# A hybrid RWKV/NSA decoder step: one ring of weight buffers for three stages, and a down projection with the weights stationary

## What is computed

```
h  = RMSNorm(x) * (1 + scale1(c)) + shift1(c)
P  = h @ w_in            # RWKV-7 columns | NSA columns | two merge gates (2 x 1024 columns)
yA = RWKV7(P_rwkv) @ w_pa ;  yB = NSA(P_nsa) @ w_pb
x  = x + gate1(c) * ((sigmoid(gA) * yA + sigmoid(gB) * yB) @ w_o)
h2 = RMSNorm(x) * (1 + scale2(c)) + shift2(c)
val, gate = split(h2 @ ffn_w_up)          # 1024 -> 2 x 2816
f  = (silu(conv3(gate)) * val) @ ffn_w_down   # 2816 -> 1024
x  = x + gate2(c) * f
```

## Time and profile before

| | us |
|---|---|
| median of 3 runs | 2840.73 |
| the profiled execution | 2833.18 |
| its span | 2831.5 |
| first merge matmul | 1534.13 |
| first up matmul | 2000.81 |
| first down matmul | 2524.47 |
| start of the last down matmul | 2828.37 |

### The profile page before, as it was taken

How to read it: one execution, slowest core, us unless ns; L and a number is a source line. 1 busy time by engine, 2 the same in 40 slices (tenths; PEclk the granted TensorE clock), 3 DMA queues, 4 the chain that set the end, 5 groups by cost and what they waited for, 6 DMA issues and landing times. The chain is left out here.

```text
span 2831.5 us, 47908 instructions
## 1 busy us (share of the span) xinstructions
PE 2524.0 (89%) x20071; PEld 2054.6 (73%) x20071; DVE 1179.9 (42%) x2457; ACT 699.4 (25%) x1400; POOL 384.2 (14%) x284
## 2 busy tenths in 40 slices
PE   4896998999857898989986999999799999979999
PEld 2675885454434676868585888744799999979999
DVE  5331224555512444435363011134233333359998
ACT  3231124566411213222222000011111111113333
POOL 3001200000120000000002111000222233223320
PEclk6897987999868989999997999999899999989999
DMA  7434411101332000000002101031211111122210
GB/s 266 183 135 133 140 35 43 31 1 46 105 119 76 17 6 24 7 23 3 12 3 102 27 26 31 9 126 55 57 50 49 45 45 45 45 95 73 70 49 16
DMA packets 150472, 171.45 MB, mean 61 GB/s; under 512 B 14089, under 2 KB 135242, under 8 KB 147762
## 3 DMA queue, kind: packets, MB, share of 16 engines
q1 hardware_dynamic: 144626, 152.66, 16.7%
q0 software_dynamic: 5632, 15.74, 1.9%
HBM read 155.47 MB, written 17.05 MB: 61 GB/s over the span
## 5 line engine op out<-in xcount | busy, mean ns | idle before, releaser
L173 PE MATMUL pP_u<-h_hi,w_up_hi 128*128 128x352 f32 x1056 | 341.5, 323 | 11.8 <-POOL w_up_lo L167 11.8
L174 PE MATMUL pP_u<-h_lo,w_up_hi 128*128 128x352 f32 x1056 | 339.2, 321 | 0.0
L175 PE MATMUL pP_u<-h_hi,w_up_lo 128*128 128x352 f32 x1056 | 338.8, 321 | 0.0
L173 PE MATMUL pP_d<-w_down_hi,a_piece_hi 128*128 128x256 f32 x792 | 226.4, 286 | 31.1 <-DVE a_piece_lo L2911 31.1
L174 PE MATMUL pP_d<-w_down_lo,a_piece_hi 128*128 128x256 f32 x792 | 225.3, 284 | 0.0
L175 PE MATMUL pP_d<-w_down_hi,a_piece_lo 128*128 128x256 f32 x792 | 225.1, 284 | 0.0
L173 PEld LDWEIGHTS pP_u<-h_hi,w_up_hi 128*128 128x128 f32 x1056 | 198.8, 188 | 11.9 <-POOL w_up_lo L167 11.9
L174 PEld LDWEIGHTS pP_u<-h_lo,w_up_hi 128*128 128x128 f32 x1056 | 199.0, 188 | 0.0
L175 PEld LDWEIGHTS pP_u<-h_hi,w_up_lo 128*128 128x128 f32 x1056 | 198.5, 188 | 0.0
L1584 PE MATMUL pB_e<-hT,w_rwkv 128*128 128x352 f32 x576 | 182.3, 473 | 16.7 <-DVE rw_slots L1608 9.5
L2801 DVE TENSOR_TENSOR conv<-conv,conv_sig 128x1056 f32<-128x1056 f32 x22 | 50.4, 2289 | 322.8 <-ACT conv_sig L2769 322.8
(11 more groups left out here) (468 smaller groups left out, 4741.5 us busy)
## 6 DMA issues: line engine op xcount, KB each, us to landing
w_up<-in_w_up SPq DMA_DIRECT2D x44, 512.0 KB, 4.1
ybT<-in_w_ada SPq DMA_DIRECT2D x9, 2048.0 KB, 7.6
kv_ring<-in_pool_kv SPq DMA_DIRECT2D x80, 128.0 KB, 2.1
xt<-in_x SPq DMA_DIRECT2D x16, 512.0 KB, 3.7
cx<-in_pool_c POOLq DMA_DIRECT2D x64, 128.0 KB, 3.0
cx<-in_pool_c SPq DMA_DIRECT2D x64, 128.0 KB, 2.9
w_gate<-in_w_in SPq DMA_DIRECT2D x16, 512.0 KB, 4.2
w_rwkv<-in_w_in SPq DMA_DIRECT2D x14, 512.0 KB, 4.1
```

The costliest lines, as they stand in the source:

```text
L173: nc.tensor.matmul(out, w_hi, x_hi, start=start, stop=False)
L174: nc.tensor.matmul(out, w_hi, x_lo, start=False, stop=False)
L175: return nc.tensor.matmul(out, w_lo, x_hi, start=False, stop=stop)
```

## The change

One set of buffers (`w_raw` for what a transfer brings, `w_hi` and `w_lo` for the parts, two slots of 128 x 1024 each) is made before the last RWKV stage, in the memory that some RWKV tensors held before. The gate blocks are numbers 0 to 15 of one sequence, the up blocks 16 to 59 (`UP0`), the down blocks from 60 on (`DOWN0`). Load n waits until block n-2 is split; the split of n waits until PE has used n-2, or stands in a stage that begins after that.

Blocks 0 and 1 are loaded and split in the last RWKV stage. Merge loads blocks 2 to 17 and splits 2 to 16; out_proj splits 17 and loads 18 and 19; up loads 20 to 61 and splits 18 to 60; down does the rest.

In the down projection blocks of 128 x 128 weights are stationary and 352 tokens stream past. A quarter of 256 columns is two halves of 128, and it is cut in 6 parts (five of 4 blocks of FF, one of 2). A piece is a part and 352 tokens; there are 72. The sums of a quarter stay in 6 PSUM banks over its 6 parts. They come out as columns by tokens, so ACT copies them to SBUF (`f_cols`), PE transposes them, two 128 x 128 blocks to an output of 256 columns (a turn), and DVE multiplies by the gate and adds. A turn stands after each half piece in the first two parts of the next quarter; the nine turns of the last quarter stand at the end. The gate rows are waited for at the first output.

```diff
+def load_block(sp, S, n, source):
+    if n >= 2:
+        sp.wait_ge(S["w_split"], 2 * (n - 1))
+    rows, width = source.shape[1:]
+    dst = S["w_raw"][:, n % 2, 0:rows * width].rearrange("p (k n) -> p k n", n=width)
+    sp.dma_start(dst, source).then_inc(S["w_in"][n % 2], 16)
+
+def split_block(nc, pool, S, n, size=1024):
+    pool.wait_ge(S["w_in"][n % 2], 16 * (n // 2 + 1))
+    x = slice(0, size)
+    split(nc, nc.gpsimd, S["w_raw"][:, n % 2, x], S["w_hi"][:, n % 2, x], S["w_lo"][:, n % 2, x], S["w_split"], 2 * n)
+
+UP0, DOWN0 = 16, 16 + 2 * FC
+DOWN_Q = 256
+DOWN_PART = [(0, 4), (4, 8), (8, 12), (12, 16), (16, 20), (20, 22)]
...
 # last stage of rwkv
                 @block.sync
                 def _(sp):
+                    for g in range(2):
+                        load_block(sp, S, g, gate_block(A, g))
                     sp.dma_start(O["shift"], R["last"][:, :, :]).then_inc(done, 16)
                     sp.wait_ge(done, 16)
+
+                @block.gpsimd
+                def _(pool):
+                    for g in range(2):
+                        split_block(nc, pool, S, g)
 # merge
-                sp.dma_start(WG[:, 0], A["w_in"][:, :, G0:G0 + 128]).then_inc(wg_in[0], 16)
                 for w, n in enumerate(("w_pa", "w_pb")):
                     sp.dma_start(WP[:, w], A[n]).then_inc(wp_in, 16)
-                for g in range(1, 16):
...
+                for g in range(2, 16):
+                    load_block(sp, S, g, gate_block(A, g))
+                for n in range(2):
+                    load_block(sp, S, UP0 + n, up_block(A, n))
...
+                for g in range(2, 17):
+                    pool.wait_ge(mm, 2 * (g - 2) + 1)
+                    split_block(nc, pool, S, g)
 # out_proj
                 for i in range(10):
+                    if i in (4, 6):
+                        load_block(sp, S, UP0 + i // 2, up_block(A, i // 2))
...
+            @block.gpsimd
+            def _(pool):
+                split_block(nc, pool, S, UP0 + 1)
 # ffn_up
+                for n in range(4, 2 * FC):
+                    load_block(sp, S, UP0 + n, up_block(A, n))
+                for n in range(2):
+                    load_block(sp, S, DOWN0 + n, down_block(A, n))
...
+                for n in range(2, 2 * FC + 1):
+                    pool.wait_ge(mm, n - 1)
+                    split_block(nc, pool, S, UP0 + n)
 # ffn_down, order of the turns
+        for m, (n, i) in enumerate(pieces):
+            h, k = chunks[n]
+            for half in range(2):
+                turn_after[m, half] = waiting.pop(0) if waiting else None
+            if k == 0 and h:
+                waiting += [9 * (h - 1) + 3 * i + c for c in range(3)]
+        last_turns = list(range(9 * (NQ - 1), 9 * NQ))
 # ffn_down, POOL
+                for n, (h, k) in enumerate(chunks[1:], 1):
+                    if n == 1:
+                        pool.wait_ge(S["up_mm"], 2 * FC)
+                    else:
+                        pool.wait_ge(mm, 3 * (n - 1))
+                    split_block(nc, pool, S, DOWN0 + n, Q * (PART[k][1] - PART[k][0]))
 # ffn_down, ACT, after the hi part of piece m
+                    if m >= 2 and chunks[pieces[m - 2][0]][1] == NK - 1:
...
+                        nc.scalar.activation(fT[:, j % 3, :, :], pP[:, i, :, 0:PIECE], ACT.Copy).then_inc(evicted, 1)
 # ffn_down, PE
+                def turn(r):
+                    j, (c0, w) = r // 3, CUTS[r % 3]
+                    pe.wait_ge(evicted, j + 1)
+                    if r >= 2:
+                        pe.wait_ge(gated, r - 1)
+                    for half in range(2):
+                        last = nc.tensor.transpose(pT[0:w, r % 2, 128 * half:128 * half + 128], fT[:, j % 3, half, c0:c0 + w], S["ident"])
+                    last.then_inc(turned, 1)
...
+                    for half in range(2):
+                        for f in range(b - a):
+                            last = split_product(nc, pP[:, i, half, 0:PIECE], block_part(S, DOWN0 + n, Q * f + 128 * half),
+                                                 [x[:, m % 3, f, :] for x in AR], k == 0 and f == 0, k == NK - 1 and f == b - a - 1)
+                        if half == 1:
+                            last.then_inc(mm, 1)
+                        if turn_after[m, half] is not None:
+                            turn(turn_after[m, half])
+                for r in last_turns:
+                    turn(r)
 # ffn_down, DVE
+                for m, (n, i) in enumerate(pieces):
+                    if m >= 2:
+                        for half in range(2):
+                            if turn_after[m - 2, half] is not None:
+                                output(turn_after[m - 2, half])
...
+                    nc.vector.tensor_tensor(AR[1][:, m % 3, 0:b - a, :], aT[:, a:b, PIECE * i:PIECE * i + PIECE],
+                                            AR[0][:, m % 3, 0:b - a, :].bitcast(F32), ALU.subtract).then_inc(lo_done, 1)
+                for r in last_turns:
+                    output(r)
```

More of the change, by code:

```diff
@@ L2713, in ffn_up @@
         pP = ctx.enter_context(nc.psum_tensor("pP_u", [128, 2, 3, 512], F32))
-        w_in = [sem(f"wup_in{k}") for k in range(2)]
-        w_split = sem("wup_split")
-        prev_in, zero, mm, gate_in, val_in, conv, sig, act_done, chain = (
-            sem(f"fu_{n}") for n in ("prev", "zero", "mm", "gate", "val", "conv", "sig", "done", "chain"))
+        mm = S["up_mm"] = sem("fu_mm")
+        prev_in, zero, gate_in, val_in, conv, sig, act_done, chain = (
+            sem(f"fu_{n}") for n in ("prev", "zero", "gate", "val", "conv", "sig", "done", "chain"))
         par = S["par"]
@@ L2844, in store_rows @@
                 def store_rows(h):
-                    for i, (t0, m) in enumerate(TILES):
-                        sp.wait_ge(added, NT * (4 * h + 3) + i + 1)
-                        sp.dma_start(y[t0:t0 + m, h * Q:(h + 1) * Q], rows[0:m, h % 2, i, :]).then_inc(S[f"y_out{h % 2}"], 16)
+                    for r in range(9):
+                        sp.wait_ge(added, 9 * h + r + 1)
+                        c0, w = CUTS[r % 3]
+                        t0 = PIECE * (r // 3) + c0
+                        sp.dma_start(y[t0:t0 + w, h * Q:(h + 1) * Q], rows[0:w, h % 2, r, :]).then_inc(S[f"y_out{h % 2}"], 16)
@@ L2857, in _ @@
                         load_rows(0)
                         load_rows(1)
-                    if k == 3 and h >= 1:
+                    if k == NK - 1 and h >= 1:
                         store_rows(h - 1)
@@ L2891, in _ @@
                     if i == 0:
-                        pe.wait_ge(w_split, 2 * (n + 1))
-                    if m >= 8:
-                        pe.wait_ge(gated, m - 7)
+                        pe.wait_ge(S["w_split"], 2 * (DOWN0 + n + 1))
+                    if k == 0 and h:
+                        pe.wait_ge(evicted, 3 * (h - 1) + i + 1)
                     pe.wait_ge(lo_done, m + 1)
-                    for f in range(b - a):
-                        last = split_product(nc, pP[:, m % 8, 0:Q], [x[:, m % 3, f, :] for x in AR],
-                                             [x[:, n % 3, f, :] for x in WR], f == 0, f == b - a - 1)
@@ new lines, in output @@
+                def output(r):
+                    j, w = r // 3, CUTS[r % 3][1]
+                    h = j // 3
+                    gate = gates[1 if r % 9 == 8 else 0][0:w, h * Q:(h + 1) * Q]
+                    if r == 0:
+                        dve.wait_ge(gate_in, 48)
+                    if r % 9 == 0:
+                        dve.wait_ge(x_in[h % 2], 48 * (h // 2 + 1))
+                    dve.wait_ge(turned, r + 1)
+                    if r >= 2:
+                        dve.wait_ge(added, r - 1)
+                    nc.vector.tensor_tensor(gated_rows[0:w, r % 2, :], pT[0:w, r % 2, 0:Q], gate, ALU.mult).then_inc(gated, 1)
+                    dve.wait_ge(gated, r + 1)
+                    x = rows[0:w, h % 2, r % 9, :]
+                    nc.vector.tensor_tensor(x, gated_rows[0:w, r % 2, :], x, ALU.add).then_inc(added, 1)
```

177 lines of the change are left out of this document (76 added, 101 removed).

## The result

| | runs | median us | lowest to highest |
|---|---|---|---|
| before | 4 | 2841.62 | 2837.29 to 2843.26 |
| changed | 4 | 2774.72 | 2773.57 to 2783.27 |

The ratio is 0.977 (95% interval 0.9751 to 0.9796): 66.9 us less, where 60.2 were forecast. Five more runs on another chip had a median of 2774.90 us and a ratio of 0.9771 (0.9758 to 0.9784).

What follows compares the result with a forecast made beforehand. PE, busy 89% of the span, and its idle holes before merge, up and down were taken as the bound. Gains 12.8 + 8.6 + 6.0 + 39.4 less 6.6 make 60.2 us: 2840.7 to 2780.5, said as 2780, range 2769 to 2793.

Steps and rivals of the forecast that it cites:

- merge start: First merge matmul near 1520.8 instead of 1534.13, with gate blocks loaded and split a stage early: 13.3 us gained.
- given back in the first gate block: In merge, PE may wait for the second w_pab transfer: 0 to 1.2 us lost, taken as 0.5.
- up start: First up matmul near 1992.2 instead of 2000.81, with the first up blocks split earlier: 8.6 us gained.
- down start: First down subtraction no longer behind the gate rows, but stretched 0 to 2.3 us by POOL (1.4 taken): 6.0 us gained.
- down's body: Down's matmul stream with weights stationary: 264.8 us instead of 304.2, 39.4 us gained.
- end: After down's last matmul, nine turns and nine outputs remain: 9.5 us instead of 2.85, 6.6 us lost.
- 27 turns: Pairs of transposes inside down's matmul stream: 5.9 to 15.1 us in all, taken as 0.3 each, 8.1 us.
- three collisions and three quarter starts: In down, POOL splits meeting an output and its subtraction (1 us each), late quarter starts (about 0.2 each): 3.5 us.
- Starved pieces: Rival, 11%: in down PE waits more for ACT and DVE because POOL splits stretch subtractions; gain 46 us, time 2795.
- Head starts given back: Rival, 5%: other traffic or a stage end replaces the removed waits of merge and up; gain 39 us, time 2802.
- Turns on DVE: Rival, 3%: in down, turns and next pieces wait on DVE's queue; even at 62 us, up to 33 us slower, 2873.
- Clock: Rival, 2%: transposes in down's stream keep PE at its lower clock level; 47 us lost, time 2827.

Runs made afterwards that it cites:

- gate rows first: The changed kernel with one wait put back: DVE waits for the gate rows before its first subtraction in down; 2776.99 us (one run).
- late split: The changed kernel, but POOL splits down block 1 only after DVE's first three subtractions; 2769.07 us (one run), repeated 2771.68 us, ratio 0.9764 to before.
- no head starts: The changed kernel with the first blocks of merge, up and down loaded and split in that stage itself; 2804.04 us, ratio 0.9871 to before.
- ring only: The changed kernel's shared weight buffers and early loads and splits for merge and up, with the old down projection; 2819.16 us, ratio 0.992 to before.
- subtraction first: The changed kernel, but DVE makes each piece's lo subtraction ahead of the outputs of two pieces before; 2776.39 us (one run).
- turns twice: The changed kernel with each pair of PE transposes in down issued twice, the second over the first; 2776.39 us (one run).

## Why the prediction was right

| step | forecast us | measured us (profile) |
|---|---|---|
| merge start | -13.3 | -13.2 |
| given back in the first gate block | +0.5 | +1.2 |
| up start | -8.6 | -8.7 |
| down start | -6.0 | -5.4 |
| down's body | -39.4 | -40.2 |
| end | +6.6 | +6.8 |
| last RWKV stage (from its store to merge) | 0 | +1.0 |
| rest of merge, out_proj, rest of up | 0 | +0.1 |
| sum (measured: unrounded) | -60.2 | -58.5 |

The repeated profile of the changed kernel has 1274.3 us from that store on, 61.0 less than before. So the intervals lie close to the 60.2 us of the forecast. By the runs the gain is 66.9 and 66.4 us: the profiled run of before lies 7.5 us below its first median, and in what part of its other runs these are is not known, since there is one profile of it. If its 1335.3 us from the store on held for a run at the median, 2841.62, the store would stand at 1504.6 us (an estimate), as late as in the latest of all thirteen profiles (1493.5 to 1504.6). So a few us may lie behind the store too, and the forecast doesn't explain them.

**The merge start** came as worked out from the load, the split and their cover. The first gate block gave back 1.2 us, but not for the reason given: PE shows no wait for w_pab there, so that the forecast had put 0.5 us at this place was luck. The windows show what it was: 14 matmuls in the first 4 us at 0.50, and in the next 3 us still 0.73; 19 matmuls ran at the lower level, 10 before.

```profile
1530.20:1534.20 4.00, 3.99 (x14) 4.00 (x15) 4.00 (x10) 4.00 (x12) 0.00 (x0) 0.50 0.83 332
1534.20:1537.20 3.00, 3.00 (x16) 3.00 (x16) 3.00 (x8) 3.00 (x9) 0.00 (x0) 0.73 1.00 421
```

In the repeated profile of the same kernel it was 10 again and the block took 13.0 us, 0.1 more than before, so this is scatter of the execution and no cost of the change. The last RWKV stage's 1.0 us is of the same kind: it took 23.5 us before, 24.4 in this profile and 23.8 in the repeated one.

**The down start** rested on two statements, and both held: the wait for gate rows bound it (gate rows first: 9.4), and the split of block 1 stretches the subtraction. The size of the second was taken at 1.4 us and is 2.0 (late split). A third the prediction leaves unsaid: the load had to be a stage early as well, or the split would have bound it at 9.2 (no head starts). The Trainium skill (GPSIMD Engine Reference, 1. Specifications) says that GpSimd shares SBUF interfaces with VectorE and that instructions with two SBUF inputs contend; this case's traces agree, with 3.82 us against 1.57.

**The body.** Its terms, forecast and then read from the spacing of the matmuls in the changed kernel's profile:

| term | forecast us | measured us |
|---|---|---|
| 1584 matmuls at 0.1585 | 251.1 | 251.1 |
| start at the lower level | 2.1 | 2.0 |
| 27 turns | 8.1 | 6.1 |
| three collisions and three quarter starts | 3.5 | 3.8 |
| pitch 0.1591 instead of 0.1585, and the last matmul's own length | 0 | 1.0 |
| sum | 264.8 | 264.0 |

The turns were the mis-sized term: forecast at 0.3 each, measured 0.226; the bubble of a late wait that I had put in at a part of them is missing, since outputs run ahead. The profile shows no wait of PE at a turn in the stream. The stalls were right in place, number and size: 0.94 for a collision (forecast 1) and 0.29 for a quarter start (forecast 0.2). The pitch was read slightly wrong: of the 631 matmuls of the window in the earlier trace rows, two began ahead of it, so 629 begin in 100 us, one per 0.159 us. That the turns' error and the pitch's cancel in part is luck; the sum is off by 0.8 us, and the turns alone by 2.0.

**The rivals.** Starved pieces: PE did wait for subtractions that POOL had stretched, but for 2.8 us and not 10. Head starts given back: refuted by ring only, where the first matmuls of merge and up come as early and 20.8 us are gained, and by no head starts, which is 29 us slower than the changed kernel. Turns on DVE: the queue order is real, and subtraction first shows what it costs, 2.3 us and not the 62 that would have used up the gain. Clock: the granted clock is 1.00 in all three windows that hold the turns, and in turns twice a second pair adds 0.216 us. The Trainium skill (TensorE: Matmul & The Clock Gate, Part 4: PE-mode transpose) states that the full clock doesn't engage for transpose-mode matmuls; here single pairs among matmuls at the upper level took nothing from it, so what the rival drew from the rule, a lower clock for the whole stream, isn't so. Whether a row of transposes alone would hold the upper level no run here shows, and the trace lists the pairs as MATMUL and doesn't say in which mode they ran. The trace of out_proj, with 1.00, pointed the same way.

## What to carry to other kernels

Read what ends the idle time ahead of each stage's first matmul, and then what would end it next. Where load and split of the first block were that wait, moving them a stage early was worth 8.7 and 13.2 us. In down a DMA wait stood ahead of the first instruction that didn't need it, and the block's load was next in line: either moved alone gave 1.1 or 1.4 us, both together 5.4. Price a matmul stream by pitch times count: tokens as the moving side took away a nearly empty tile's matmuls (32 rows at the price of 128), by the sum some 24 of the 40 us (not tested by itself), for 0.23 us per transposed pair. An edit that makes the first piece shorter makes the next one due sooner: look whose instructions lie beside it, before counting the gain.

## What was not expected of the hardware

The time that TensorE spends at its lower level after a stage's start differs from execution to execution of one program: the same first matmuls of merge took 19 at that level in one profile of the changed kernel and 10 in the other (5.66 and 3.04 us). For matmuls of 352 columns it lies between 10 in 3.0 us and 21 in 6.3 us over all profiles, which is worth up to 1.5 us a stage. What it goes with is not settled: ahead of down a PE idle for some 12.5 us had 13 to 19 such matmuls, one idle for 10.3 to 10.4 us had 16 to 21, and one idle for 16.4 to 16.6 us (no head starts, gate rows first) 15 and 11. Differences of 1 us or so between single profiles can be this alone. A wait in the middle of a stage can bring the lower level back: in ring only it did so twice, behind 2.17 and 1.74 us of idle PE, for about 1.5 us each time.

The unchanged first 1500 us differ by as much as 11 us between profiles (store issued at 1493.5 and at 1504.6); the two profiled runs of the changed kernel differ by 9.4 us in span, and 6.8 of these lie there. It hides a gain of 2 us unless intervals inside the profile are compared.
